# Mixer order rearranged in a two-layer hybrid encoder on one core: index sums, low weight parts, query turns

## The reference

```python
xn = rmsnorm(xp, norm_mix[l])
q, k, v, qi, ki, wi, u, gv = project(xn, w_in[l], pos)        # q, k, qi, ki with partial rotary
score = sum over 8 index heads of relu(qi . ki) * wi          # top-k of score picks the keys
a = attention of q over the picked keys                       # 8 heads of 64, 2 kv heads
gvn = rmsnorm(gelu(gv), gate_norm[l])
bmix = gelu(u) * spatial_mix(gvn, w_spatial[l], b_spatial[l])
x = x + concat(a, bmix) @ w_out[l]
x = x + relu(rmsnorm(x, norm_ffn[l]) @ w_ff1[l])**2 @ w_ff2[l]
```

## Time and profile before

| | us |
|---|---|
| median of 3 runs | 1450.5 |
| lowest and highest | 1446.13 and 1455.37 |
| the profiled execution | 1448.09 |
| its span, first to last instruction | 1446.3 |
| TensorE busy in it | 1363.4 (94%) |
| VectorE, ScalarE, GpSimd busy | 716.0, 515.3, 224.0 |
| mean granted TensorE clock | 0.972 |

### The profile page before, as it was taken

How to read it: one execution, slowest core, us unless ns; L and a number is a source line. 1 busy time by engine, 2 the same in 40 slices (tenths; PEclk the granted TensorE clock), 3 DMA queues, 4 the chain that set the end, 5 groups by cost and what they waited for, 6 DMA issues and landing times.

```text
span 1446.3 us, 21713 instructions
## 1 busy us (share of the span) xinstructions
PE 1363.4 (94%) x9033; PEld 1237.5 (86%) x9033; DVE 716.0 (50%) x1292; ACT 515.3 (36%) x898; POOL 224.0 (15%) x257
## 2 busy tenths in 40 slices
PE   6997878999999999999999796989999999999997
PEld 5765656899999999999986474669999999999997
DVE  4375874355444444444635579435544444444444
ACT  5365624333223123133323664344331321321322
POOL 4225334210000000000211632332000000000011
PEclk9998979999999999999999898999999999999999
DMA  5110101133223222222331101103223232222221
GB/s 173 59 59 15 45 15 32 53 100 88 79 84 87 77 85 87 76 87 74 93 99 44 44 22 35 32 16 110 74 88 86 76 88 83 79 88 75 87 73 66
DMA packets 169762, 102.34 MB, mean 71 GB/s; under 512 B 7432, under 2 KB 159936, under 8 KB 169664
## 3 DMA queue, kind: packets, MB, share of 16 engines
q1 hardware_dynamic: 169664, 100.95, 24.0%
HBM read 96.98 MB, written 3.95 MB: 70 GB/s over the span
## 4 chain that ended last, share of the span: by engine, by line
PE 89%; DVE 5%; issue 2%; POOL 2%; ACT 2%; DMA 1%; SPq 0%; ACTq 0%; POOLq 0%; DVEq 0%
PE bank L1542 64%; PE bank L1284 14%; PE bank L1391 3%; PE bank L1304 1%; PE bank L1416 1%; PE bank L1439 1%; DVE late L994 1%; DVE m L992 1%; DMA late<-in_x_prompt 1%; PE bank L1345 1%; PE bank L1319 1%; PE bank L1461 1%; PE bank L1584 0%; DVE p_lo L1085 0%; DVE late L1047 0%
## 5 line engine op out<-in xcount | busy, mean ns | idle before, releaser
L632 ACT ACTIVATE ring_hi<-ring_raw 128x1024 fp32r<-128x1024 f32 x176 | 185.0, 1051 | 276.0 <-PE bank L1542 248.7
L1542 PE MATMUL bank<-vh,ring_hi 128*128 128x288 f32 x1280 | 275.6, 297 | 2.8 <-DVE vl L1093 2.8
L1542 PE MATMUL bank<-vh,ring_lo 128*128 128x288 f32 x1280 | 275.2, 296 | 0.0
L1542 PE MATMUL bank<-vl,ring_hi 128*128 128x288 f32 x1280 | 275.2, 296 | 0.0
L892 DVE TENSOR_TENSOR ring_lo<-ring_raw,ring_hi 128x1024 fp32r<-128x1024 f32 x162 | 209.3, 1292 | 121.5 <-ACT ring_hi L632 113.7
L1542 PE MATMUL bank<-xh,ring_hi 128*128 128x288 f32 x1024 | 220.7, 297 | 1.9 <-issue 1.9
L1542 PE MATMUL bank<-xl,ring_hi 128*128 128x288 f32 x1024 | 220.2, 296 | 0.0
L1542 PE MATMUL bank<-xh,ring_lo 128*128 128x288 f32 x1024 | 220.2, 296 | 0.0
L1542 PEld LDWEIGHTS bank<-vh,ring_hi 128*128 128x128 f32 x1280 | 205.2, 189 | 3.7 <-DVE vl L1093 3.7
L1542 PEld LDWEIGHTS bank<-vh,ring_lo 128*128 128x128 f32 x1280 | 205.2, 188 | 0.0
L1542 PEld LDWEIGHTS bank<-vl,ring_hi 128*128 128x128 f32 x1280 | 205.2, 188 | 0.0
(11 more groups left out here) (193 smaller groups left out, 1548.7 us busy)
## 6 DMA issues: line engine op xcount, KB each, us to landing
ring_raw<-in_w_ff SPq DMA_DIRECT2D x128, 512.0 KB, 4.0
ring_raw<-in_w_in SPq DMA_DIRECT2D x32, 512.0 KB, 3.7
ring_raw<-in_w_out SPq DMA_DIRECT2D x32, 128.0 KB, 2.9
ring_raw<-in_w_out SPq DMA_DIRECT2D x16, 256.0 KB, 3.2
late<-in_x_prompt SPq DMA_DIRECT2D x4, 512.0 KB, 6.7
out_y_prompt<-late SPq DMA_DIRECT2D x4, 512.0 KB, 3.6
w_sp<-in_w_spatial SPq DMA_DIRECT2D x2, 512.0 KB, 4.5
gate_bc<-in_gate_norm SPq DMA_DIRECT2D x2, 256.0 KB, 5.4
```

The costliest lines, as they stand in the source:

```text
L632: s.activation(ring_hi[:, n % NSLOT, :], ring_raw[:, n % NRAW, :], ACT.Copy).then_inc(hi_ready, 1)
L1542: last = mm(bank[unit_bank(u) + half][:, 0:HALF], w[:, k, :], a[:, k, HALVES[half]], start=k == 0 and w is wh and a is ah, stop=k == KT - ...
```

## The change

Only the mixer's order changes; every product, sum and output stays. In words:

- NXV is 24: tile 2's index adds are VectorE's too; GpSimd has the last eight.
- Transposes and pairs start a step or two earlier, transposes 0 to 3 two in a step, alternating between banks 7 and 6. Query transpose 3 has bank 6.
- The copies to ki4 and the scaling to wi are ScalarE's (index_copies), after all of the KVQI evacuations.
- The rotary of the queries stands in pieces in steps 37, 39 and 40 of GpSimd's order, between the adds.
- All low parts from tile 6 on are GpSimd's; they stand in the second step of a quarter.
- Scores steps are one earlier, and the inverse sums one step behind their scores step instead of two, in VectorE's order after the masks.
- gv_norm is cut in a scaling by ScalarE (gating_scale) and a product by GpSimd (gate_gain), in steps 62 to 64.
- The split of tile 18 and the gelus of u come after p_high in step 80.
- A new table of top-k steps.

```diff
-    NXV = 2 * NIH
+    NXV = 3 * NIH
...
-    IDX0 = QUARTERS * NT + 1
-    TR_AT = {IDX0: 0, IDX0 + 1: 1, IDX0 + 2: 2, IDX0 + 3: 3, IDX0 + 7: 4, IDX0 + 9: 5, IDX0 + 11: 6, IDX0 + 13: 7}
-    PAIR_AT = {IDX0 + d: p for p, d in enumerate([5, 6, 7, 8, 9, 10, 11, 12, 14, 15, 17, 18, 20, 21, 22, 23])}
-    SCORED = dict(zip(INDEX_TILES, [IDX0 + 9, IDX0 + 13, IDX0 + 22, IDX0 + 31]))
-    QT_AT = {IDX0 + 24 + a: a for a in range(NT)}
-    QK_AT = [IDX0 + 25 + k for k in range(10)] + [IDX0 + 40 + k for k in range(8)] + [IDX0 + 50 + k for k in range(8)]
+    TR_AT = {22: [0, 1], 23: [2, 3], 27: [4], 29: [5], 31: [6], 33: [7]}
+    TR_BANK = [7, 6, 7, 6, 7, 7, 7, 7]
+    PAIR_AT = {g: p for p, g in enumerate([*range(25, 37), 37, 39, 41, 43])}
+    SCORED = dict(zip(INDEX_TILES, [29, 33, 37, 48]))
+    Q_ROPE_AT = {37: 0, 39: 1, 40: 2}
+    QT_AT = {41 + a: a for a in range(NT)}
+    QT_BANK = [7, 7, 7, 6, 7]
+    QK_AT = [*range(45, 55), *range(59, 67), *range(70, 78)]
...
-    INV = [(QK_AT[k] + 2, k, 1) for k in range(10)] + [(QK_AT[k + 1] + 2, k, 2) for k in range(10, NQ, 2)]
+    INV = [(QK_AT[k] + 1, k, 1) for k in range(10)] + [(QK_AT[k + 1] + 1, k, 2) for k in range(10, NQ, 2)]
...
-    NORM_AT = {IDX0 + 42 + a: a for a in range(NT)}
-    MIX_AT = {IDX0 + 48: 0, IDX0 + 49: 1, IDX0 + 53: 2, IDX0 + 54: 3, IDX0 + 55: 4}
+    SCALE_AT = {62: [0, 1], 63: [2, 3], 64: [4]}
+    MIX_AT = {67: 0, 68: 1, 72: 2, 73: 3, 74: 4}
...
-        d = g - IDX0
-        return (0 if d < 9 else 2 if d < 13 else 4 if d < 24 else 1 if d < 29 else 2 if d < 35 else 4 if d < 40 else
-                2 if d < 48 else 4 if d < 50 else 0)
+    FILL = [(0, 0), (29, 2), (33, 3), (37, 4), (45, 2), (55, 4), (59, 2), (67, 4), (70, 0)]
...
-        POOL_SPLITS = range(S_OUT - 4, S_OUT + NSLOT)
+        POOL_SPLITS = range(QUARTERS + NSLOT - 1, S_OUT + NSLOT)
```

On GpSimd (rope's copies go, index_add's loops go into the steps):

```diff
-                    link(rope(z, Z_QI, NIH + 1, ID, RI, rows, ts, 4 * RH))
-                    g.tensor_copy(ki4[0:rows, ts, :].rearrange("p t (o d) -> p t o d", o=4),
...
-                last.then_inc(idx_roped, 1)
+                    rope(z, Z_QI, NIH + 1, ID, RI, rows, ts, 4 * RH).then_inc(idx_roped, 1)
...
-                for s in range(QK_AT[0], END):
+                for s in range(QUARTERS * NT, END):
...
-                    if t == 0 and n + NSLOT - 1 in POOL_SPLITS:
+                    if s in Q_ROPE_AT:
+                        q_rope(Q_ROPE_AT[s])
+                    if 2 * PAIR_AT.get(s, 0) >= NXV:
+                        for i in (2 * PAIR_AT[s], 2 * PAIR_AT[s] + 1):
+                            index_add(i)
+                    if t == 1 and n < S_OUT:
                         split_lo(n + NSLOT - 1)
...
+                    for tt in SCALE_AT.get(s, ()):
+                        gate_gain(tt)
```

On ScalarE, and VectorE's wait for the new copies:

```diff
+                def gating_scale(t):
+
+                    act.wait_ge(rv_ready, l + 1)
+                    s.activation(gvn[0:ROWS[t], t, :], gvn[0:ROWS[t], t, :], ACT.Copy, scale=rv[0:ROWS[t], t:t + 1])\
+                        .then_inc(gv_scaled, 1)
...
+                    for tt in SCALE_AT.get(at, ()):
+                        gating_scale(tt)
+                    if at == QUARTERS * NT:
+                        for part in range(3):
+                            index_copies(part)
...
+                    if at == NG_IN:
+                        split_hi(N0 + S_OUT + NSLOT - 1)
+                    for a in U_EVAC.get(at, ()):
+                        evac(UU, U_ORDER[a])
...
+                    if i == 0:
+
+                        dve.wait_ge(wi_ready, 3 * (l + 1))
```

More of the change, by code:

```diff
@@ L557, in index_add, with q_rope, gate_gain @@
                     ins.then_inc(idx_acc_p, 1)
[L559 to L563, removed]
+                def q_rope(part):
+                    rows, ts = thirds[part]
+                    pool.wait_ge(proj_evac, NT * (4 * l + QQ) + ts.stop)
                     rope(q, 0, NH, HD, RH, rows, ts, 0).then_inc(q_roped, 1)
-                for i in range(NX - NIH, NX):
-                    index_add(i)
+                def gate_gain(t):
+                    pool.wait_ge(gv_scaled, NT * l + t + 1)
+                    g.tensor_tensor(gvn[0:ROWS[t], t, :], gvn[0:ROWS[t], t, :], gate_bc[0:ROWS[t], :], ALU.mult)\
+                        .then_inc(gvn_ready, 1)
                 def split_lo(n):
@@ L1124, in _ @@
                             out_low(g)
-                    for at_, k, steps in INV:
-                        if at_ == at:
-                            inverse_sums(k, steps)
                     if at == MEAN_AT:
@@ L1132, in _ @@
                         v.reciprocal(rv[:, :], mv[:, :]).then_inc(mv_ready, 1)
-                    if at in NORM_AT:
-                        if NORM_AT[at] == 0:
-                            dve.wait_ge(rv_ready, l + 1)
-                        gv_norm(NORM_AT[at])
-                    for _ in range(fill(at)):
+                    for _ in range([steps for g, steps in FILL if g <= at][-1]):
                         topk_next(at)
-                    if at in TR_AT:
-                        tr_copy(TR_AT[at])
-                        if TR_AT[at] == 5:
+                    for i in TR_AT.get(at, ()):
+                        tr_copy(i)
+                        if i == 5:
                             values_low()
@@ L1157, in _ @@
                             masked_logits(i)
+                    for at_, k, steps in INV:
+                        if at_ == at:
+                            inverse_sums(k, steps)
                     if at in T_AT:
@@ L1312, in tr_group @@
                     n = NTR * l + tr[0]
-                    if n:
-                        pe.wait_ge(tr_evac, n)
+                    prior = [m for m in range(tr[0]) if TR_BANK[m] == TR_BANK[tr[0]]]
+                    if prior:
+                        pe.wait_ge(tr_evac, NTR * l + prior[-1] + 1)
+                    elif l:
+                        pe.wait_ge(q_lo_ready, NT * l)
                     c0 = 0
@@ L1318, in tr_group @@
                         rows = src.shape[0]
-                        last = tp(bank[7][:, c0:c0 + rows], src, ident[0:rows, 0:rows])
+                        last = tp(bank[TR_BANK[tr[0]]][:, c0:c0 + rows], src, ident[0:rows, 0:rows])
                         c0 += rows
@@ L1358, in q_transpose @@
                     t = TILE_ORDER[a]
-                    pe.wait_ge(q_roped, 3 * l + (1 if t < NPT // 2 else 2 if t == SMP else 3))
+                    pe.wait_ge(q_roped, 3 * l + (1 if t < NPT // 2 else 3 if t == SMP else 2))
                     if a == 0:
                         pe.wait_ge(tr_evac, NTR * (l + 1))
+                    elif QT_BANK[a] == 6:
+                        pe.wait_ge(idx_relu, NX * (l + 1))
                     else:
-                        pe.wait_ge(q_lo_ready, NT * l + a)
+                        pe.wait_ge(q_lo_ready, NT * l + max(m for m in range(a) if QT_BANK[m] == 7) + 1)
                     for b in range(4):
-                        last = tp(bank[7][:, b * ROWS[t]:(b + 1) * ROWS[t]], q[0:ROWS[t], t, b * P:(b + 1) * P],
+                        last = tp(bank[QT_BANK[a]][:, b * ROWS[t]:(b + 1) * ROWS[t]], q[0:ROWS[t], t, b * P:(b + 1) * P],
                                   ident[0:ROWS[t], 0:ROWS[t]])
@@ L1492, in _ @@
                             small_rows()
-                    if at in TR_AT:
-                        i = TR_AT[at]
+                    for i in TR_AT.get(at, ()):
                         if i == 0:
                             pe.wait_ge(small_in, 16 * 5 * (l + 1))
-                            pe.wait_ge(idx_roped, l + 1)
+                            pe.wait_ge(ki4_ready, 3 * (l + 1))
                         if i == 4:
```

51 lines of the change are left out of this document (27 added, 24 removed).

## The result

The changed kernel takes **1427.6 us** (median of four runs, 1426.3 to 1428.7) against 1449.0 for the kernel before on the same chip: ratio 0.985, 95% interval 0.981 to 0.988. Forecast were 1418 in a range of 1400 to 1438. The time lies in the range and is faster by more than 1%, but the gain is 21 us instead of 31: a third of it didn't come. The profiled execution went from a span of 1446.3 to 1425.5 us, 20.8 less where the sum had 32.6.

The account below looks back on a forecast made before the run. TensorE, busy 94% of the span, loses time to mixer waits and half-clock stretches behind them. Gains of 16.3 us a layer, 32.6 for two, gave 1415.5; plus 2.4 for the median, 1418 us; own range 1402 to 1432, chances' range 1400 to 1438.

Parts of the forecast that it names:

- Index transposes: Step 22: TensorE's 2.2 us wait and 1.7 us of clock loss go, 3.9 us a layer gained.
- Splits on GpSimd hold adds: GpSimd's splits 7, 8 and 9 can each hold a VectorE index add: 0.8 us a layer lost, ends 0 and 7.2.
- Steps 37 to 46: Index relu, query transposes, first masks: waits 8.4 us become 4.2, clock loss 6.1 becomes 3.4; gain 6.9 a layer.
- The crumbs: Small TensorE waits at the p transposes shrink by 1.3 us a layer.
- Top-k of tile 2: Steps 55 to 60: VectorE's mask late, TensorE waits 7.1 us, 1.9 of clock behind it as before; gain 2.4 a layer.
- Gate norm: From step 62: 5.0 us saved, less a new 1.3 us wait and 1.7 of clock; gain 2.0 a layer.
- The end of the mixer: The p copy goes ahead of split, table load and gelus, which delay the next copy instead; gain 0.6 us a layer.
- rival (a): Clock gives nothing back: shorter waits still make half-clock stretches of old sizes everywhere but step 22; 1427 us, chance 0.14.
- Rival (b): GpSimd's splits hold VectorE's index adds for their whole length, 7.2 us a layer instead of 0.8; 1431 us, chance 0.08.
- Rival (c): VectorE's top-k mask of tile 2 sets the time whatever comes before, absorbing earlier gains; 1440 us, chance 0.08.
- Rival (d): ScalarE's wait for the gate's root turns steps 62 to 78 into a chain, making it slower; 1458 us, chance 0.04.
- (e): The big wait, 7.1 us plus 1.9 of clock, goes because VectorE catches up in steps 45 to 58; 1400 us, chance 0.08.

Follow-up runs that it names:

- Experiment 3: Changed kernel with weight remainders 7 to 11 given back from GpSimd to VectorE: 1429.0 us (ratio 0.986).
- experiment 12: Changed kernel with evened-out top-k turns, gelus and last split after step 81's copies, first query tile's high copy ahead of index relus 28 and 29: 1398.4 us.
- experiment 2: Changed kernel with 26 extra matmuls that nobody reads, in step 60 ahead of the scores: 1425.3 us (ratio 0.983).
- experiment 5: Changed kernel with ScalarE's last weight split and first gelus one step later, behind step 81's copies: 1420.6 us (ratio 0.981).
- experiment 6: Changed kernel with the end of the mixer in the order it had before the change: 1422.1 us (ratio 0.982).
- experiment 7: Changed kernel with the gate normalisation again as five fused VectorE operations in steps 62 to 66: 1439.8 us, very uneven.
- experiment 9: The kernel of experiment 7 with the 26 extra matmuls of experiment 2 in step 60: 1428.7 us (ratio 0.988).
- experiment 4: Changed kernel with two index tiles added by VectorE instead of three, the third scaled by ScalarE and added by GpSimd: 1431.8 us (ratio 0.988).
- experiment 11: Changed kernel with the query rotation's three parts in one row in step 40: 1432.3 us (ratio 0.989).

## Why the prediction was right in its range and too high in its gain

By its own steps:

- *Index transposes*, 2.2 + 1.7: right. No wait, and no stretch at that place.
- *Splits on GpSimd hold adds*, 0.8: right. Three operations were held (3.28 us for 1.32 in one pair), one of them reaches TensorE, and 0.9 us of step 37's wait of 1.6 goes without the splits. Experiment 3 gained nothing by that, as the next wait grew by 1.0.
- *Steps 37 to 46*: waits of 3.0 (said 2.8) in step 42 and 0.95 or 0 (said 1.4) in step 46. The chain add 25, rope 1, add 26, relu 29, q_low 0 is the one that ran, and experiment 12 cut it at the place named. The clock behind it was 1.6 in layer 0 and 4.5 in layer 1, against 3.4.
- *The crumbs*, 1.3: what steps 45 to 66 had besides the waits named shrank by 0.9 and 0.7.
- *Top-k of tile 2*: 7.2 for 7.1. The sixteen turns were there. But "1.9 of clock behind it as before" was 8.5 in layer 0 and 2.3 in layer 1: **the first term that failed**, worth 7 us in two layers. By experiment 2 only some 4 of the 8.5 were time, as the rest ran into VectorE's next masks.
- *Gate norm*: waits of 0 and 1.4 in step 65 (said 1.3); the 1.7 of clock said to be left there didn't come, which gave 3.4 back in two layers. A wait at this place came in layer 1 alone; that ScalarE's order causes it was argued and not tested.
- *The end of the mixer*, + 0.6: **the second term that failed**, and the only one wrong in sign. Idle time rose by 0.6 and 0.3 us and clock loss from 0 to 3.4 and 4.6, 8.0 us in two layers. (The part's length grew by only 2.2 and 2.9, since 2.0 us of TensorE's work had moved ahead of step 79.) I saw that 3.6 us of split, table load and gelus stand ahead of the next copy, and priced them as before. Before, they met TensorE in four pieces with no stretch behind them; now the longest is 4.4 us and two stretches follow. Experiments 5 and 6 change this place alone: their times are 7.0 and 5.5 us lower, and their traces have 5.8 and 6.3 us less from step 79 on.

So the number of rival (a), 1427, came out, though not quite its mechanism. It had half-clock stretches of the old sizes at the old places; in truth some places lost theirs, one grew, and the end got new ones. It was given 0.14, and the sentence against it ("the waits of 2.7 us near the end are not followed by one") was used to rule out what the new order brought there. Rival (b) is out by experiment 3. Rival (c) is out by the ledger: step 59 begins 8 to 10 us earlier in a layer, and step 60's wait did not take that up. Rival (d) is out by steps 67 to 78, where nothing is idle, and (e) by the 7.2 us that stayed. The signs named: no wait at the index transposes, 5.4 gone, 3.0 at 109 us, 7.2 in step 60, all seen; but group 79 is 12 and 14 us earlier instead of 16, and the mean clock 0.975, a rise that the spread of the runs covers.

That the time still lies in the range is in part luck. In two layers the clock terms missed by 7.1 us in steps 59 to 66 and by 8.0 at the end, and 3.4 in steps 67 to 78 and 0.4 before step 59 went the other way; and of the 8.5 us behind step 60 in layer 0 only 3.9 were time. The step that was wrong is the one that carries a stretch over with its wait at the old size, for one layer that is then doubled: the two layers came out different.

That the sum was right in its idle terms, to 1.9 us in two layers, and wrong in its clock terms is shown by the ledger and by experiments 2, 5, 6, 7 and 9. Why the stretch behind step 60 was so long in layer 0 is not settled; what goes with it stands in the last section.

## What to carry to other kernels

Keep idle time and clock loss in separate columns: idle time could be worked out here to 1 us a layer from the order of each engine (with misses in single terms that cancel), clock loss could not, so the range, not the sum, should hold it. When an order is rearranged, look at how idle time is grouped and not only at its total: the end's 6.4 us, with no piece over 2.7, came with no clock loss before and 5.7 us with pieces up to 2.9 with 1.7 in experiment 6, while 6.8 with 4.4 in one piece came with some 4. In single layers it varies by more than that. And count a planner's background turns against the tile that is due first: moving one tile's start from step 48 to 57, with two small shifts, gave 17.6 us, nearly as much as the whole change.

## What the runs showed of the hardware that I had not expected

**The same wait, very different stretches.** Step 60's wait is 7.2 us in fourteen profiled layers (the changed kernel and experiments 3, 4, 5, 6, 7 and 11), behind the same instructions. The granted clock around it was 0.50 for 20.5 and 6.8 us in the changed kernel's two layers, 6.8 twice in experiment 3, 6.8 and 17.1 in 4, 5 and 6, 17.1 and 10.2 in 11, and 30.7 twice in 7:

```profile
167.60:174.40 6.80, 3.67 (x9) 2.64 (x9) 5.71 (x18) 1.37 (x5) 0.00 (x0) 0.50 0.00 0
853.60:870.70 17.10, 13.44 (x30) 8.73 (x30) 11.43 (x32) 7.82 (x16) 6.19 (x9) 0.50 0.07 21
```

(experiment 5, layer 0 and layer 1.) In the stretch TensorE was busy in nearly all of the time after the wait; in the changed kernel's layer 0, from the end of the wait on:

```profile
170.10:187.10 17.00, 17.00 (x38) 10.58 (x39) 9.81 (x28) 10.39 (x21) 9.77 (x12) 0.50 0.11 31
```

So work behind a wait doesn't by itself bring the clock back at once. What goes with the length, in all fourteen layers, is when in the wait the clock fell. It fell 4.1 to 5.1 us after the wait began in the six layers with 6.8 us, 3.4 to 3.8 us after it in the seven with 17.1 us or more (3.8 and 5.0 in the changed kernel's two), and 2.3 us after it in the one with 10.2. No experiment moved that moment on purpose, so this is what the traces have in common and not a cause shown. The run times follow the mean clock: of experiment 7's five runs the one at 0.985 took 1425.8 us and the one at 0.966 took 1443.6.

**Half clock can be free.** With the stretch prevented, layer 1's steps 59 to 66 went from 31.4 to 31.15 us, though 2.3 us of clock loss had gone (experiment 2): TensorE then waited for VectorE instead.

**GpSimd's hold on VectorE, sized.** VectorE's two adds of 128x384 took 3.28 us beside GpSimd's split of 128x1024 and 1.32 without. The Trainium skill (SBUF — State Buffer, "Who interferes with whom") has the two engines exclude each other for a whole instruction in such a pair, and the rows agree. The price for TensorE was far less than the 7.2 us a layer that three whole blocks would give: 0.9 us in step 37, and no more idle time over steps 20 to 44 as a whole (4.6 us a layer with the splits on GpSimd, 4.7 without).
